# Three transposition banks and one sum bank in the attention stage, and first operands made while the last projection unit still runs

## The chip, the cores and the metric

One core of a Trainium2 chip runs the whole kernel. The metric is the device time of one launch in microseconds (us), the median over several executions. Engines are called as the profile calls them: PE is TensorE's matrix array and PEld its weight loads, ACT is ScalarE, DVE is VectorE, POOL is GpSimd, SP is the queue that issues most transfers. PSUM, where PE writes, has eight banks of 128 partitions by 512 float32.

## The reference, cut to what matters

One layer of a decoder for 1024 tokens of 1024 channels. What the change touches is the projection and the attention:

```python
h = rmsnorm(x, norm_mix_g)
proj = h @ w_in        # q | k_c v_c | k_s v_s | k_w v_w | gates | conv b, c, u
# 8 heads of 64 in 2 key/value groups; per query three branches:
#   compressed blocks (63 of them), selected blocks (all 16, so plain causal), window of 512
s = q*scale @ k.T - slope * distance;  p = masked_softmax(s);  o_branch = p @ v
o_attn = g0 * o_c + g1 * o_s + g2 * o_w
x = x + [rmsnorm(o_attn) | rmsnorm(o_conv)] @ w_out
x = x + (silu(dwconv3(h2 @ w_gate) + b) * (h2 @ w_up)) @ w_down     # h2 = rmsnorm(x)
```

## The kernel before, in words

**Precision.** Large matrix products run in a fast float32 form. An operand is split into a high part (an ACT copy that rounds) and a low part (a DVE subtraction of the high part from the operand), and products are summed over the parts. So every operand that is made costs an ACT instruction and then a DVE instruction that waits for it.

**Projection.** `w_in` is cut into 23 units of 128 output columns, numbered 0 to 22. A unit is 8 tiles (`unit_tile`, L486 to L496) of 6 matmuls each, one tile for each 128 rows of the contraction. All units read the normalised input from `R1`: tile `kt` reads `R1[kt]` (high) and `R1[8 + kt]` (low). A unit writes a pair of banks, number `n % 3`, and `evac` (L1276) on DVE multiplies it out of PSUM. Units 12 to 15 are queries, 16 the gates, 17 and 18 the compressed keys and values, 19 and 20 keys and values of group 0, 21 and 22 those of group 1. Between units 21 and 22 PE does the hidden layer of the compression.

**Attention operands.** `QA`, `QB`, `KA`, `KB`, `VT1`, `VT2`, `EX` lie in `R1`, the memory that the projection reads; `VT0` and group 1's keys lie in the weight slots `wh`, `wl`. `QA` holds queries (high and low), `QB` queries again with 20 rows of position terms below them, which two POOL transfers bring for queries and keys (L803, L804). Each engine makes its share (POOL L792, ACT L968, L976, L978, L987, L993, DVE L1367, L1368, L1381, L1387, L1394). In the kernel before, all of it waits for the end of unit 22 (`unit_done >= N_IN`), since any of it may lie in a slot that unit 22 still reads. DVE makes the low queries of heads 1 to 3 and the low values between the first four row maxima.

**Attention.** Work comes in blocks of 128 queries of one group (`BLOCKS`, 26 of them), 4 units each (one for a head; 104 units). For unit U: PE computes scores (L1831, L1832, masks L1843) into bank pair `U % 2` (banks 0 to 3), DVE takes row maxima (L1421), ACT exponentials (L1033). `scores(U)` waits for the exponentials of U - 2. While the units of a block run, each engine also handles the steps of the block before it, interleaved by `steps_behind`. A step is one tile of 128 keys for the four heads; there are 148 steps in 48 groups, and a group is one branch of one row of blocks. For step s PE transposes exponentials (L1879, 4 of them) into a ring of banks, ACT copies the high part out (L1044), DVE makes the low part (L1462, which frees the bank, semaphore `t_used`), and two steps later PE multiplies with the values (L1899, L1900) into the group's sum bank. When the group is complete, ACT copies the sum out (L1051), PE transposes it back (L1908) in a bank of the same ring, DVE adds the halves (L1448), and POOL weighs and adds the branches (L822, L827, L830). In the kernel before, banks 4 and 5 are the ring and banks 6 and 7 alternate as sum bank:

```python
PV_LAG, COPY_LAG, TURN_LAG, SQUARE_LAG = 2, 3, 6, 10
# turn_step(s):  pe.wait_ge(t_used, at - 1)        L1877
# values(s):     pe.wait_ge(t_used, T_OF[s] + 1)   L1887
#                pe.wait_ge(ot_copied, group - 1)  L1889, first step of a group
```

The order on every engine is fixed by these loops. A lag L means: done when step s + L is handled. Behind the attention, PE starts the output projection, whose tiles partly cover the last group's way out.

Of the kernel before, what the change touches and what calls it, by code (L numbers as in the profile page):

```python
# [27 lines left out]
ALU = mybir.AluOpType  # L28
# [3 lines left out]
P = 128  # L32
D = 1024
T = 1024
# [120 lines left out]
PV_LAG, COPY_LAG, TURN_LAG, SQUARE_LAG = 2, 3, 6, 10  # L155
# [18 lines left out]
PLAIN = [False for _ in STEPS]  # L174


def split_upto(s):
    return PLAIN[:s + 1].count(False)


def plain_before(s):
    return max([k + 1 for k in range(s) if PLAIN[k]], default=0)


# [19 lines left out]
def hybrid_layer(nc, xT, w_units, w_cmp1, w_cmp2, params_d, consts_d, masks_d, alibi_q, alibi_k, outT):  # L204
    with ExitStack() as ctx:
# [81 lines left out]
        VT1 = piece((2 * TT + 1) * P).rearrange("p (j d) -> p j d", d=P)  # L287
        VT2 = piece(2 * P).rearrange("p (j d) -> p j d", d=P)
        EX = piece(2 * BANK).rearrange("p (a b) -> p a b", a=2)
# [21 lines left out]
        EP = F1[:, K0 + 2, 0:BANK]  # L311
# [46 lines left out]
        x_in, aq_in = [sem(f"x_in{k}") for k in range(KT)], sem("aq_in")  # L358
# [409 lines left out]
        def _(pool):  # L768
# [15 lines left out]
            pool.wait_ge(unit_done, N_IN)  # L784

            def query_tiles(g, half, h):
                tiles = slice(half * TT // 2, (half + 1) * TT // 2)
                return tiles, F1[0:DH, Q0 + 2 * g + h // 2, :].rearrange("p (i q) -> p i q", q=P)[:, tiles, :]

            def queries_again(g, half, h):  # L790
                tiles, src = query_tiles(g, half, h)
                nc.gpsimd.tensor_scalar(QB[0:DH, tiles, h, :], src, DH ** -0.5, None, ALU.mult).then_inc(qb_even, 1)  # L792

            def queries(g, half, h):

                tiles, src = query_tiles(g, half, h)
                if g:
                    pool.wait_ge(sc_ready, FREE_Q[1 + half])
                nc.gpsimd.tensor_scalar(QA[0:DH, tiles, h, :], src, DH ** -0.5, None, ALU.mult).then_inc(qp_hi, 1)
# [1413 lines left out]
```

## Time and profile before

| what | value |
|---|---|
| time of the kernel before, median of 3 runs | 1434.09 us (1432.82 to 1435.97) |
| profiled execution, its own time | 1430.31 us |
| its span, first to last instruction | 1428.5 us |
| mean granted TensorE clock | 0.978 |
| PE busy | 1327.5 us, 93% |
| DVE busy | 868.8 us, 61% |
| ACT busy | 577.7 us, 40% |
| POOL busy | 332.3 us, 23% |
| attention, first scores to last values | 294.39 to 624.85 us |

The profile shows one execution. Engines run side by side, so busy shares do not add up to the span. A wait is put down to the instruction that came last. The granted clock is 1.00 where PE runs at 2.4 GHz and 0.50 where it runs at 1.2 GHz; a stretch with a number between has some of each. Matmul durations are those of one instruction from start to end; back to back, matmuls overlap, and the distance of their starts is what a sequence of them costs.

### The profile page before, as it was taken

How to read it: one execution, taken by the hardware profiler on the slowest of the kernel's cores; microseconds unless marked ns; L12 is line 12 of the kernel's file. 1: busy time of each engine (PE TensorE's matmuls, PEld its weight loads, DVE VectorE, ACT ScalarE, POOL GpSimd, SP SyncE). 2: the span in 40 equal slices, each digit the busy share in tenths (PEclk: the TensorE clock that was granted, in tenths of full speed). 3: DMA queues.
4: the chain of work that ended last, by engine and by line, in shares of the span. 5: the costliest groups of instructions: out<-in, count | busy, mean ns of one | idle time of the engine just before them, and what ended most of it. 6: DMA issues, size and time to landing. Idle time of an engine off the chain costs nothing.

```text
span 1428.5 us, 17091 instructions
## 1 busy us (share of the span) xinstructions
PE 1327.5 (93%) x6366; PEld 1078.7 (76%) x6366; DVE 868.8 (61%) x1195; ACT 577.7 (40%) x1028; POOL 332.3 (23%) x247
## 2 busy tenths in 40 slices
PE   7999999968688889879997999999999999999996
PEld 6788888856566667657886788888888878888885
DVE  6333432178677888755338877777888873335442
ACT  6211111067666876734154333333333333334330
POOL 0001000032121221110036554455554510002010
PEclk9999999979989999999998999999999999999998
DMA  5111111000000000043210222122222228444631
GB/s 214 51 44 59 45 59 74 0 19 1 1 1 1 1 1 1 1 177 104 88 45 30 103 89 84 64 89 89 89 89 89 74 86 320 169 128 145 217 100 59
DMA packets 37917, 110.75 MB, mean 78 GB/s; under 512 B 3988, under 2 KB 4500, under 8 KB 37652
## 3 DMA queue, kind: packets, MB, share of 16 engines
q1 hardware_dynamic: 37552, 108.83, 21.6%
q0 software_dynamic: 288, 0.90, 0.3%
q8 instruction: 48, 0.79, 0.2%
q14 instruction: 29, 0.24, 0.1%
HBM read 90.01 MB, written 19.92 MB: 77 GB/s over the span
## 4 chain that ended last, share of the span: by engine, by line
PE 69%; DVE 16%; ACT 7%; issue 7%; DMA 1%; POOL 1%; DVEq 0%; ACTq 0%; SPq 0%; POOLq 0%
PE PS L491 8%; PE PS L492 8%; PE PS L495 8%; PE PS L2019 6%; PE PS L2021 6%; PE PS L2020 6%; PE PS L2031 6%; PE PS L2033 6%; PE PS L2032 6%; DVE wl L1551 3%; DVE nmax L1421 3%; PE PS L1879 3%; ACT F L1033 2%; DVE ER L1462 2%; ACT ER L1044 1%
## 5 line engine op out<-in xcount | busy, mean ns | idle before, releaser
L491 PE MATMUL PS<-R,wh 128*128 128x512 f32 x560 | 222.4, 397 | 13.9 <-DVE wl L483 13.9
L492 PE MATMUL PS<-R,wh 128*128 128x512 f32 x560 | 219.8, 392 | 0.0
L2019 PE MATMUL PS<-R,wh 128*128 128x512 f32 x480 | 188.7, 393 | 13.4 <-DVE wl L1551 8.3
L2020 PE MATMUL PS<-R,wh 128*128 128x512 f32 x480 | 187.5, 391 | 0.0
L2021 PE MATMUL PS<-R,wl 128*128 128x512 f32 x480 | 187.5, 391 | 0.0
L495 PE MATMUL PS<-R,wl 128*128 128x512 f32 x560 | 173.5, 391 | 0.0
L2031 PE MATMUL PS<-R,wh 128*128 128x512 f32 x352 | 137.5, 390 | 0.0
L2033 PE MATMUL PS<-R,wl 128*128 128x512 f32 x352 | 137.0, 389 | 0.0
L2032 PE MATMUL PS<-R,wh 128*128 128x512 f32 x352 | 137.0, 389 | 0.0
L491 PEld LDWEIGHTS PS<-R,wh 128*128 128x128 f32 x560 | 106.0, 189 | 37.8 <-DVE wl L483 14.7
L495 PEld LDWEIGHTS PS<-R,wl 128*128 128x128 f32 x560 | 106.1, 189 | 22.6
L492 PEld LDWEIGHTS PS<-R,wh 128*128 128x128 f32 x560 | 106.1, 189 | 22.4 <-issue 0.7
L2019 PEld LDWEIGHTS PS<-R,wh 128*128 128x128 f32 x480 | 90.6, 189 | 36.5 <-DVE wl L1551 11.6
L1153 ACT ACTIVATE wh<-F 128x512 fp32r<-128x512 f32 x110 | 67.5, 625 | 111.2 <-PE PS L2021 99.5
L1879 PE MATMUL PS<-consts,F 128*128 128x128 f32 x528 | 84.2, 283 | 25.7 <-DVE ER L1462 7.5
L2021 PEld LDWEIGHTS PS<-R,wl 128*128 128x128 f32 x480 | 90.5, 189 | 19.0
L2020 PEld LDWEIGHTS PS<-R,wh 128*128 128x128 f32 x480 | 90.7, 189 | 18.5
L1421 DVE TENSOR_REDUCE nmax<-PS 128x1 f32<-128x64 f32 (+6 forms) x192 | 96.0, 538 | 13.5 <-PE PS L1843 12.1
L1551 DVE TENSOR_TENSOR wl<-F,wh 128x512 fp32r<-128x512 f32 x110 | 92.7, 851 | 5.0 <-ACT wh L1153 5.0
L1033 ACT ACTIVATE F<-PS,nmax 128x640 f32<-128x640 f32 (+7 forms) x128 | 89.2, 702 | 8.1 <-DVE nmax L1421 7.9
L1462 DVE TENSOR_TENSOR ER<-PS,ER 128x512 fp32r<-128x512 f32 (+1 forms) x99 | 68.1, 688 | 38.4 <-ACT ER L1044 37.1
L822 POOL TENSOR_TENSOR PBm<-PBm,factor 128x256 f32<-128x256 f32 x48 | 29.4, 613 | 265.8 <-DVE PBm L1448 265.4
(222 smaller groups left out, 2454.0 us busy)
## 6 DMA issues: line engine op xcount, KB each, us to landing
raw<-in_w_units SPq DMA_DIRECT2D x70, 512.0 KB, 3.6
F<-in_w_units SPq DMA_DIRECT2D x32, 512.0 KB, 4.1
gated<-F SPq DMA_DIRECT2D x22, 512.0 KB, 2.6
F<-gated SPq DMA_DIRECT2D x44, 256.0 KB, 3.6
F<-in_xT SPq DMA_DIRECT2D x16, 512.0 KB, 9.0
F<-in_w_units SPq DMA_DIRECT2D x12, 384.0 KB, 3.2
residual<-F SPq DMA_DIRECT2D x8, 512.0 KB, 2.6
F<-residual SPq DMA_DIRECT2D x8, 512.0 KB, 6.3
```

What stands on the lines that cost most here:

```text
L491: nc.tensor.matmul(out, w_h, hi(kt)[:, cols], start=first, stop=False)
L492: nc.tensor.matmul(out, w_h, lo(kt)[:, cols], start=False, stop=False)
L495: last = nc.tensor.matmul(out, w_l, hi(kt)[:, cols], start=False, stop=end)
L1421: last = nc.vector.tensor_reduce(nmax[:, br, i, h:h + 1], pair(U % 2)[:, col:col + count], AX.X, ALU.max, negate=True)
L1551: nc.vector.tensor_tensor(product_slot(wl, n), block_of(m, PRODUCTS[q][0]), f32(product_slot(wh, n)), ALU.subtract)\
L1879: last = nc.tensor.transpose(PS[0:rows, 4 + at % 2, h * P:(h + 1) * P], e_cols(n, br, h, j), ident)
L2019: nc.tensor.matmul(out, w_h, operand(name, k, 0), start=fresh and k == 0, stop=False, skip_group_check=not fresh)
L2020: nc.tensor.matmul(out, w_h, operand(name, k, 1), start=False, stop=False, skip_group_check=not fresh)
L2021: last = nc.tensor.matmul(out, w_l, operand(name, k, 0), start=False, stop=k == 3, skip_group_check=not fresh)
L2031: nc.tensor.matmul(out, w_h, a_part(n, 0), start=first, stop=False)
L2032: nc.tensor.matmul(out, w_h, a_part(n, 1), start=False, stop=False)
L2033: return nc.tensor.matmul(out, w_l, a_part(n, 0), start=False, stop=end)
```

## The change

Two edits in one. First, the banks: exponentials are transposed into a ring of three banks (4, 5, 6), and a single bank (7) collects the sums of every group. The lags of copying out, transposing back and squaring become 2, 4 and 8, and ACT copies a group's sum out before the exponentials of that place and not behind them. Second, the last projection unit: value transposes for group 0 move ahead of unit 22, the compressed values' matmuls into it, and unit 22 counts each finished tile in `r1_free`. `R1` is laid out anew, query pieces are split in halves, so that the first query half is free after 3 tiles (`Q_FREE`), group 0's keys after 5 (`K_FREE`), and the last values after 7 (`V2_FREE`). ACT, DVE and POOL make the first queries, keys and values at these counts. DVE multiplies unit 22 out (`evac(22)`) behind them. The transfer of the query rows is split in two, the second behind unit 22. A switch that was off everywhere (`PLAIN`) goes.

```diff
-PV_LAG, COPY_LAG, TURN_LAG, SQUARE_LAG = 2, 3, 6, 10
+PV_LAG, COPY_LAG, TURN_LAG, SQUARE_LAG = 2, 2, 4, 8
+T_RING, T_BANK, O_BANK = 3, 4, 7
...
-        QA = piece(GROUP * T).rearrange("p (i h q) -> p i h q", h=GROUP, q=P)
-        QB = piece(GROUP * T).rearrange("p (i h q) -> p i h q", h=GROUP, q=P)
-        KA = [piece(KEYS), flat(wh[:, :, :])[:, 0:KEYS]]
-        KB = [piece(KEYS), flat(wl[:, :, :])[:, RING * 1024 - KEYS:]]
+        def tiles_read(start, end):
+            return max(c // 1024 % KT for c in range(start, end)) + 1
+
+        QA, QB, KA, KB = [], [], [], []
+        QA.append(query_piece())
+        KA.append(piece(KEYS))
+        K_END = at_r[0]
+        QA.append(query_piece())
+        VT1 = piece((2 * TT + 1) * P).rearrange("p (j d) -> p j d", d=P)
+        QB_START = at_r[0]
+        QB.append(query_piece())
+        Q_FREE = max(tiles_read(0, GROUP * T // 2), tiles_read(QB_START, at_r[0]))
+        KB.append(piece(KEYS))
+        K_FREE = max(tiles_read(GROUP * T // 2, K_END), tiles_read(at_r[0] - KEYS, at_r[0]))
+        QB.append(query_piece())
...
@@ gpsimd
-            pool.wait_ge(unit_done, N_IN)
-            pool.wait_ge(qkv_ready, 4)
-            pool.dma_start(flat(QB[DH:DH + 2 * AR, :, :, :].rearrange("r i h q -> r i (h q)")), alibi_q).then_inc(aq_in, 16)
-            pool.dma_start(KB[0][DH:DH + 2 * AR, :], alibi_k[0]).then_inc(ak_in[0], 16)
-            queries_again(0, 0, 0)
-            for g in range(KV):
+            pool.wait_ge(qkv_ready, 2)
+            pool.wait_ge(r1_free, Q_FREE)
+            query_rows(0)
+            queries_again(0, 0, 0)
             queries_again(0, 0, 2)
+            pool.wait_ge(r1_free, K_FREE)
+            pool.dma_start(KB[0][DH:DH + 2 * AR, :], alibi_k[0]).then_inc(ak_in[0], 16)
+            key_pads(0)
+            pool.wait_ge(unit_done, N_IN)
+            query_rows(1)
+            key_pads(1)
             pool.dma_start(KB[1][DH:DH + 2 * AR, :], alibi_k[1]).then_inc(ak_in[1], 16)
@@ scalar
-            act.wait_ge(unit_done, N_IN)
+            act.wait_ge(qkv_ready, 8)
+            values_hi(slice(0, 2))
+            act.wait_ge(r1_free, Q_FREE)
+            for h in range(GROUP):
+                queries(0, 0, h)
+            act.wait_ge(r1_free, K_FREE)
             for half in range(2):
                 keys(0, half, 0)
-            queries(0, 0, 0)
             compressed_keys(0)
-            for h in range(1, GROUP):
-                queries(0, 0, h)
-            values_hi()
+            act.wait_ge(r1_free, V2_FREE)
+            act.wait_ge(v_lo, 2)
+            values_hi(slice(2, 3))
+            compressed_values()
@@ scalar, copy_out and behind
-                nc.scalar.activation(OT[group % 2], PS[:, 6 + group % 2, :], ACT.Copy).then_inc(ot_copied, 1)
+                nc.scalar.activation(OT[group % 2], PS[:, O_BANK, :], ACT.Copy).then_inc(ot_copied, 1)
                 if s < NS:
                     split_step(s)
+                if s - COPY_LAG in LAST_OF:
+                    copy_out(LAST_OF[s - COPY_LAG])
                 if unit is not None:
                     exponentials(unit)
                 if s in VALUES_AT:
                     later_values_hi(s)
-                if s - COPY_LAG in LAST_OF:
-                    copy_out(LAST_OF[s - COPY_LAG])
@@ vector
-            evac(22, 0, 0, 0, F1[:, 10, :])
+            values_lo(slice(0, 2))
+            for h in range(GROUP):
+                queries(0, 0, h)
             for half in range(2):
                 keys(0, half, 0)
-            queries(0, 0, 0)
             compressed_keys(0)
+            evac(22, 0, 0, 0, F1[:, 10, :])
...
-                if U < 3:
-                    queries(0, 0, U + 1)
                 if U == 1:
-                    values_lo()
-                if U == 2:
+                    values_lo(slice(2, 3))
                     compressed_values()
@@ tensor
-            pe.wait_ge(masks_in, 16)
+            pe.wait_ge(qkv_ready, 9)
             for t in range(TT):
                 last = nc.tensor.transpose(PS[:, 4 + t // 4, (t % 4) * P:(t % 4 + 1) * P], F1[:, V0, t * P:(t + 1) * P], ident)
             last.then_inc(vt_ready, 1)
+            pe.wait_ge(unit_lo, N_IN)
+            for kt in range(KT):
+                last = unit_tile((N_IN - 1) % RING, (N_IN - 1) % 3, h_hi, h_lo, kt, kt == 0, kt == KT - 1)
+                last.then_inc(unit_done if kt == KT - 1 else r1_free, 1)
+                if kt == 4:
+                    compressed_values()
@@ tensor, scores
                 if U == 0:
-                    pe.wait_ge(aq_in, 16)
-                    pe.wait_ge(clear_ready, 2 * KV)
+                    pe.wait_ge(aq_in[0], 16)
+                    pe.wait_ge(qkv_ready, N_QKV - 1)
+                if U == 1:
                     pe.wait_ge(qkv_ready, N_QKV)
@@ tensor, turn_step and turn_out
-                    pe.wait_ge(t_used, at - 1)
+                    pe.wait_ge(t_used, at - T_RING + 1)
@@ tensor, values
-                if s == first and group > 1:
-                    pe.wait_ge(ot_copied, group - 1)
-                elif s == first and group == 1:
+                if s == first and group:
+                    pe.wait_ge(ot_copied, group)
+                elif s == first:
                     pe.wait_ge(vc_lo, KV)
-                out, v = PS[:, 6 + group % 2, :], value_tile(g, br, j)[rows, :]
+                out, v = PS[:, O_BANK, :], value_tile(g, br, j)[rows, :]
```

## Rows read from the trace of the kernel before

**Rows 1.** Windows: stretch, its length, busy PE, PEld, DVE, ACT, POOL (counts), clock, DMA.

```profile
288.00:308.00 20.00, 9.73 (x51) 8.20 (x50) 13.27 (x33) 11.30 (x39) 10.48 (x13) 0.56 0.16 34
...
312.00:626.00 314.00, 263.36 (x1658) 203.45 (x1657) 242.14 (x456) 221.87 (x536) 62.19 (x84) 0.97 0.00 1
```

**Rows 2.** Timeline 276 to 295 us: start, duration, engine, line [idle before it].

```profile
276.09 0.50 PE L491 MATMUL PS<-R,wh 128*128 128x512 f32 x1
...
287.15 1.03 PE L1797 MATMUL PS<-consts,F 128*128 128x128 f32 x8
...
287.42 1.23 DVE L1279 TENSOR_TENSOR F<-PS,F 128x1024 f32<-128x1024 f32 x1 [9.35 <-PE PS L495]
...
290.55 1.52 POOL L792 TENSOR_SCALAR R<-F 64x512 fp32r<-64x512 f32 x1
290.66 1.08 DVE L1368 TENSOR_TENSOR R<-F,R 64x512 fp32r<-64x512 f32 x1
...
294.39 0.50 PE L1831 MATMUL PS<-R 128*128 128x192 f32 x1 [6.21 <-DMA R<-in_alibi_k]
```

**Rows 3.** The chain that ended last, 295 to 306 us: start, duration, what.

```profile
295.81 0.62 DVE nmax L1421 x3
...
296.46 0.70 DVE R L1381
...
297.21 0.53 PE PS L1831
...
304.98 0.32 ACT EC L1033
305.30 0.71 ACT F L1033 x4
```

**Rows 4.** Single lines of code: count, duration min/median/max in ns, first and last start.

```profile
L976 ACT ACTIVATE R<-F x10: 626/627/630, 288.7 to 493.0; 64x512 fp32r<-64x512 f32 x10
...
L1381 DVE SCALAR_TENSOR_TENSOR R<-F,R x16: 684/685/1128, 291.8 to 499.8; 64x512 fp32r<-64x512 f32 x16
...
L1051 ACT ACTIVATE F<-PS x48: 580/598/647, 317.6 to 624.9; 128x512 f32<-128x512 f32 x48
```

**Rows 5.** Transfers issued from 280 to 300 us: KB each, us from issue to landing.

```profile
R<-in_alibi_k POOLq DMA_DIRECT2D x1, 165.0 KB, 5.7
wl<-in_alibi_k POOLq DMA_DIRECT2D x1, 165.0 KB, 3.3
```

**Rows 6.** Timeline of PE: the first scores of unit 4 and of unit 8.

```profile
304.05 0.62 PE L1831 MATMUL PS<-R 128*128 128x320 f32 x1
...
313.36 0.47 PE L1831 MATMUL PS<-R 128*128 128x448 f32 x1 [0.87 <-ACT F L1033]
```

**Rows 7.** What PE waited for, 312 to 626 us: us in total, times, longest.

```profile
PE PS L1879 <- DVE ER L1462: 12.7, 15, 2.4
...
PE PS L1879 <- DVE R L1401: 5.2, 2, 3.4
PE PS L1899 <- ACT F L1051: 4.8, 5, 1.9
...
PE PS L1908 <- DVE R L1462: 0.7, 3, 0.4
```

**Rows 8.** Timeline at 398 to 400 us, where one group's sums end and the next begin.

```profile
398.54 0.60 ACT L1044 ACTIVATE ER<-PS 128x512 fp32r<-128x512 f32 x1 [0.17 <-PE PS L1879]
398.57 0.39 PE L1900 MATMUL PS<-ER,VT 128*128 128x512 f32 x1
...
399.33 0.50 PE L1899 MATMUL PS<-R 63*128 63x512 f32 x1
```

**Rows 9.** Windows of 2 us each, columns as in rows 1.

```profile
336.00:338.00 2.00, 2.00 (x9) 1.53 (x8) 1.70 (x3) 1.38 (x3) 0.00 (x0) 0.50 0.00 0
...
382.00:384.00 2.00, 0.25 (x4) 0.21 (x3) 1.02 (x2) 1.44 (x4) 0.00 (x0) 1.00 0.00 0
...
424.00:426.00 2.00, 2.00 (x9) 1.60 (x8) 0.69 (x2) 1.62 (x4) 1.92 (x3) 0.50 0.00 0
```

More of the change, by code:

```diff
@@ L173 @@
 KEYS_DONE = 34
[L174 to L182, printed above, removed]
 def steps_behind(unit):
@@ L357, in hybrid_layer @@
                                                        sem("tapr_ready"))
-        x_in, aq_in = [sem(f"x_in{k}") for k in range(KT)], sem("aq_in")
+        x_in, aq_in = [sem(f"x_in{k}") for k in range(KT)], [sem("aq_in0"), sem("aq_in1")]
+        r1_free = sem("r1_free")
         x1_in, out_done = sem("x1_in"), sem("out_done")
@@ L975, in queries @@
                 src = F1[rows, Q0 + 2 * g + h // 2, :].rearrange("p (i q) -> p i q", q=P)[:, tiles, :]
-                nc.scalar.activation(QA[rows, tiles, h, :], src, ACT.Copy, scale=DH ** -0.5).then_inc(q_hi, 1)
+                nc.scalar.activation(QA[half][rows, :, h, :], src, ACT.Copy, scale=DH ** -0.5).then_inc(q_hi, 1)
                 if h % 2:
-                    nc.scalar.activation(QB[0:DH, tiles, h, :], src, ACT.Copy, scale=DH ** -0.5).then_inc(qb_odd, 1)
+                    nc.scalar.activation(QB[half][0:DH, :, h, :], src, ACT.Copy, scale=DH ** -0.5).then_inc(qb_odd, 1)
             def hidden(kv):
@@ L1043, in split_step @@
                     act.wait_ge(pv_done, s - ER_RING + 1)
-                nc.scalar.activation(EH[s % ER_RING][rows, :], PS[rows, 4 + T_OF[s] % 2, :], ACT.Copy).then_inc(hi_ready, 1)
+                nc.scalar.activation(EH[s % ER_RING][rows, :], PS[rows, T_BANK + T_OF[s] % T_RING, :], ACT.Copy).then_inc(hi_ready, 1)
             def copy_out(group):
@@ L1380, in queries @@
                     dve.wait_ge(qp_hi, later)
-                nc.vector.scalar_tensor_tensor(QA[other, tiles, h, :], F1[rows, Q0 + 2 * g + h // 2, :]
+                nc.vector.scalar_tensor_tensor(QA[half][other, :, h, :], F1[rows, Q0 + 2 * g + h // 2, :]
                                                .rearrange("p (i q) -> p i q", q=P)[:, tiles, :], DH ** -0.5,
-                                               f32(QA[rows, tiles, h, :]), ALU.mult, ALU.subtract).then_inc(q_lo, 1)
+                                               f32(QA[half][rows, :, h, :]), ALU.mult, ALU.subtract).then_inc(q_lo, 1)
             def compressed_keys(g):
@@ L1793, in _ @@
                     last.then_inc(gt_ready, 1)
-            pe.wait_ge(masks_in, 16)
-            for t in range(TT):
-                last = nc.tensor.transpose(PS[:, 4 + t // 4, (t % 4) * P:(t % 4 + 1) * P], F1[:, V0, t * P:(t + 1) * P], ident)
-            last.then_inc(vt_ready, 1)
             def compressed_values():
@@ L1805, in compressed_values @@
                 last.then_inc(kvc_ready, 1)
+            pe.wait_ge(qkv_ready, 9)
+            for t in range(TT):
+                last = nc.tensor.transpose(PS[:, 4 + t // 4, (t % 4) * P:(t % 4 + 1) * P], F1[:, V0, t * P:(t + 1) * P], ident)
+            last.then_inc(vt_ready, 1)
+            pe.wait_ge(unit_lo, N_IN)
[4 more added lines that the diff above has]
+                    compressed_values()
+            pe.wait_ge(masks_in, 16)
             def scores(U):
@@ L1830, in part @@
                     out = PS[:, bank, col:col + count]
-                    nc.tensor.matmul(out, QA[:, i, h, :], KA[g][:, key:key + count], start=True, stop=False)
-                    return nc.tensor.matmul(out, QB[0:DH + 2 * AR, i, h, :], KB[g][0:DH + 2 * AR, key:key + count], start=False,
+                    nc.tensor.matmul(out, QA[i // WT][:, i % WT, h, :], KA[g][:, key:key + count], start=True, stop=False)
+                    return nc.tensor.matmul(out, QB[i // WT][0:DH + 2 * AR, i % WT, h, :], KB[g][0:DH + 2 * AR, key:key + count], start=False,
                                             stop=not masked)
@@ L1894, in values @@
                 rows = slice(0, NCMP if br == CMP else P)
-                out, v = PS[:, 6 + group % 2, :], value_tile(g, br, j)[rows, :]
-                if PLAIN[s]:
-                    nc.tensor.matmul(out, f32(v), EP[rows, :], start=s == first, stop=s == end).then_inc(pv_done, 1)
-                    return
+                out, v = PS[:, O_BANK, :], value_tile(g, br, j)[rows, :]
                 nc.tensor.matmul(out, v, EH[s % ER_RING][rows, :], start=s == first, stop=False)
```

71 lines of the change are left out of this document (36 added, 35 removed).

## The prediction, made before the changed kernel was built or run

> **What bounds the kernel now.** The page comes first: PE is busy 93% of the span, so time is won only where PE idles or runs at half clock. Windows over the attention stage say where that is. From 288 to 308 us PE is busy 9.7 of 20 us at a mean clock of 0.56; from 312 to 626 us it is busy 263.4 of 314 us, so it idles 50.6 us, while DVE is busy 77% and ACT 71% [rows 1]. No engine is full there, so the stage is held by waits for one another as much as by work. Then the timeline of the first stretch: projection and value transposes end at about 288.2 us, and the first scores start at 294.39 us, released by the position rows of the keys [rows 2]. Behind them the chain of waits goes round three engines, scores on PE, maxima on DVE, low queries of the next head on DVE, scores again, and a round is 294.39 to 297.21, 2.82 us [rows 2, 3]. Last the list of what PE waited for from 312 to 626 us: seven rows (transposes L1879 and L1908 behind DVE, the first and last of them are shown) make 43 waits of 35.3 us in all. They are waits for a transposition bank. Five waits, 4.8 us, are for the copy of a group's sum [rows 7].
>
> **The front, step by step.** Unit 22 is 48 matmuls from 276.09 to 287.15 us, 11.06 us or 1.38 us a tile; the eight transposes last 1.03 us [rows 2]. In the new order transposes run from 276.1, the unit from 277.1, and the four small matmuls of the compressed values inside it are taken as 0.3 us (fewer and smaller than the eight transposes). Three tiles are done at 281.3, five at 284.0, the unit at 288.5. PE therefore finishes its part when it did before, and nothing is lost there.
>
> ACT makes four high queries and two copies, 6 x 0.63 us [rows 4], from 281.4 to 285.2, then two halves of keys to 286.5, compressed keys and values to about 287.7. DVE follows each: the low queries are done at about 285.9. Both key halves on DVE lasted from the end of its evacuation, 287.42 + 1.23, to 290.66 + 1.08, or 3.1 us [rows 2]; from 285.8, when the first high half exists, they end at 288.9, the compressed ones at 289.1. POOL issues the query rows at 281.4 (0.6), copies two heads (1.5 to 1.7 each, one shown [rows 2]) and issues the key rows at 285.2. Alone, such a transfer of 165 KB took 3.3 us; behind the 320 KB of queries 5.7 [rows 5]. The queries' half is issued 3.8 us earlier, so I take 3.3: landed at 288.5. Before, the key rows were issued as the transposes ended, at 288.2, took 5.7, and the first scores started at 294.39, 0.5 us after landing [rows 2, 5]. Two paths so meet at 289.1; the first scores start 5.3 us earlier.
>
> Then DVE has to do the evacuation of unit 22, which it used to do first: 289.1 + 1.2 = 290.3. Behind it stand the first maxima, and unit 1's scores wait for it too. From there maxima 0.65, exponentials 1.03 (0.32 + 0.71) [rows 3]: unit 2's scores start at 292.0. No low query stands between maxima any more, so a round of two units is scores 0.71 (they lay 1.42 us, 294.39 to 295.81, at half clock), maxima 0.62, exponentials 1.03, handing over 0.1: 2.5 us. Unit 4's scores start at 294.5 and not at 304.05 [rows 6]: 9.6 us. Units 4 to 7 took 9.3 us, to 313.36 [rows 6], mostly at half clock; ACT then sets their pace, and I credit two scores on the chain at full clock, 2 x 0.71 = 1.4. **The front gives 11.0 us.**
>
> This rests on the clock staying up. PE fell to half clock after it had idled 6.2 us. Later it fell about 334 to 339, 369 to 373, 392 to 397 and 421 to 427 us, each time behind a wait of 1.9 to 3.4 us; five windows of 2 us show 0.50, first and last are in rows 9. In the window 382 to 384 PE was busy 0.25 of 2 us and the clock stayed [rows 9]. In the new front no wait should be over 1 us. If it falls all the same, each of two rounds is 0.7 longer and the 1.4 is lost: 8.2 us. That is the lower bound of the front; the upper one, with evacuation not in the way, 12.2.
>
> At one place a rule speaks against this front. POOL's query copies now lie beside DVE's low queries. In the trace a subtraction on DVE that began 0.11 us after such a POOL copy took 1.08 us, and the median of the low queries is 0.685, so it cost 0.4 us and did not last to the copy's end (290.55 + 1.52) [rows 2, 4]. I go by that. The Trainium skill (SBUF — State Buffer, Who interferes with whom) says that a DVE instruction with two SBUF inputs and a GpSimd one that reads SBUF block each other for the whole instruction. By that rule DVE's low queries would wait for both POOL copies, to 285.2, and the front would give about 9 us where the rows give 11.0.
>
> **The ring of three.** Before, `turn_step(s)` waits for the same low part as `values(s - 2)` right behind it. With a third bank the four transposes go ahead and the wait meets the values. So a wait shrinks by no more than four transposes issued back to back, 0.47 us, estimated as half of eight (1.03) [rows 2] less the overlap of their ends. 43 waits x 0.47 would be 20 us; many are shorter, and with each cut at 0.47 they add up to 16 us. Not all of it stays: PE that comes earlier meets ACT and DVE still at work. DVE's 77% leaves room, so I keep somewhat over half, 9 us. Bounds 0 and 16.
>
> **One sum bank.** Waits for the copy (4.8 us [rows 7]) had the copy stand three steps behind and behind exponentials; it moves ahead of both, and I take 4 of them as gone. In return each group's first sum waits for the copy of the group before, 47 times. How long is read at each boundary: last sum ends 398.96, ACT's high part that stands ahead of the copy ends 399.14, copy 0.6 [rows 4, 8], so 399.77, and the next sum started at 399.33: 0.44 us late [rows 8]. Worked out so at all 47 boundaries, 7 are late, 3.1 us in all; at the others scores or a transposition back lie between and cover the copy by 0.1 to 2.7 us. With PE's other waits gone cover shrinks: I take 5 us. Were every boundary as bare as this one, it would be 47 x 0.44 = 21 us. That is the upper bound, 3 the lower. The copy ahead of the exponentials holds these up by 0.6 us where a unit begins; the scores behind them rarely wait for it, and I take 1 us. Moving POOL's and DVE's ends of a group two steps forward costs nothing: their instructions are the same, and POOL is idle most of the stage. The later values (L1401, 5.2 us in two waits [rows 7]) are among the 43.
>
> **Clock in the stage.** Four dips of some 4 to 6 us at half clock cost about half of each, 8 to 10 us together. The one at 369 us stands behind a wait for a copy (1.9 us [rows 7]) that should vanish, others get shorter: 3 us, bounds 0 and 6. The end of the attention is the same chain as before, with the one boundary of 0.2 us more.
>
> **Sum.** 11.0 + 9 + 4 - 5 - 1 + 3 - 0.2 = 20.8 us, from the profiled execution's 1430.31 us to 1409.5. That execution lay 3.8 us under the median of 1434.09; with the same difference on the median the forecast is 1413 us.
>
> **Rivals.** (1) Both parts pay, as above: chance 0.6, 1403 to 1421 us. (2) Only the front pays; the ring's waits move whole to the values and what the copy gives, the single bank takes: 1434 - 11 = 1423, range 1420 to 1427, chance 0.18. For it: in-order PE waits at the values for the very low part it waited for before. Against: DVE and ACT idle a quarter of the stage, partly waiting for those transposes. Its neighbour in the Trainium skill (TensorE: Matmul & The Clock Gate, HAM oscillation) is a kernel in which more PSUM buffering gave nothing; here 43 waits for a bank are in the trace, so I give it no more. (3) The front is made too late: POOL and DVE block each other, key rows land late and the clock falls behind the gap. Front 6, stage 8: 1420, chance 0.08. (4) The clock stays at full through the whole stage and the front: 10 us more from (1), 1403 or less, down to 1396, chance 0.09. (5) Slower: the single bank holds PE at every boundary for the whole copy path. The gains to be eaten are 11 + 9 + 4 + 3 = 27 us, so it decides from 27 / 47 = 0.57 us a boundary; with high part and copy both in the way (0.6 + 0.6 less 0.2 of transposes not covered) it is 1.0 x 47 = 47 us, 1454 us. Against it: the 0.44 at a bare boundary. Chance 0.05.
>
> **Numbers.** Cases 1, 3, 4 and most of 2 lie from 1401 to 1427; this is the range, with 0.1 outside on each side. A measurement tells 0.2%, 2.9 us, from no change. Faster 0.91, within 0.2% 0.05 (front at its low bound and the bank at 20 us), slower 0.04.
>
> **What would show it.** Right: first scores at 289 us, unit 4's at 294 to 295, clock 1.00 from 288 to 312; the 35.3 us of waits for a bank down to under half, those of the values for DVE up; waits of L1899 for L1051 under 6 us; the stage from unit 8 to the last values shorter by some 9 us. Wrong: a gap of several us before the first scores with half clock behind it; L1899 waiting for L1051 at most of 47 boundaries; a stage as long as before with its waits only renamed.

## The result, and the profile after

The changed kernel takes 1391.12 us (median of 4 runs, 1389.27 to 1392.53) against 1433.45 us for the kernel before (4 runs, 1432.53 to 1435.97) on the same chip: ratio 0.9701, interval 0.9682 to 0.972, or 42.3 us less. The forecast was 1413 us, and the time lies under its range. The profiled execution took 1392.53 us, against 1430.31 for the profiled one before: these two are 37.8 us apart and not 42.3, as the one before lay under its median and this one over it. What follows splits the 37.8. First the page: busy times and the granted clock over 40 slices.

```profile
PE 1318.5 (95%) x6366; PEld 1076.2 (77%) x6366; DVE 863.5 (62%) x1195; ACT 576.2 (41%) x1028; POOL 332.6 (24%) x248
...
PEclk9999999999999999999999999999999999999998
```

Then windows over the front and the stage (columns as in [rows 1]). The stage here runs from the first to the last values, 302.48 to 585.35 us; before, 311.79 to 624.85.

```profile
288.00:308.00 20.00, 15.61 (x99) 12.85 (x98) 14.52 (x45) 14.01 (x53) 6.92 (x8) 0.83 0.08 20
292.00:296.00 4.00, 2.54 (x18) 2.25 (x18) 1.55 (x9) 3.17 (x18) 4.00 (x3) 0.86 0.09 15
296.00:300.00 4.00, 3.98 (x20) 3.33 (x19) 3.16 (x11) 2.30 (x9) 0.30 (x1) 0.50 0.00 0
302.48:585.35 282.87, 253.74 (x1656) 201.36 (x1653) 236.83 (x456) 219.50 (x534) 62.43 (x84) 0.99 0.00 1
```

The same for the stage of the kernel before, from its own first values to its last:

```profile
311.79:624.85 313.06, 262.42 (x1656) 202.69 (x1653) 242.14 (x456) 221.47 (x535) 62.19 (x84) 0.97 0.00 1
```

The first values start 9.3 us earlier, and the stage is 30.2 us shorter. Its 1656 matmuls are the same, so the 30.2 split in two: PE idles 29.1 us and not 50.6 (21.5 less), and is busy 253.7 us and not 262.4 (8.7 less). What follows the stage is 1.8 us longer. How much of the 8.7 is the clock can be read: windows over the stretches in which the granted clock was 0.50, their sum for the kernel before (four stretches) and for ring_of_two below (six), the one stretch of the changed kernel, and the sum of its second profiled execution, after_again (two):

```profile
sum 17.00, PE 15.80 PEld 12.98 DVE 10.05 ACT 8.30 POOL 3.16; mean PE 3.95 PEld 3.24 DVE 2.51 ACT 2.07 POOL 0.79
sum 20.60, PE 20.00 PEld 17.33 DVE 12.66 ACT 9.73 POOL 4.76; mean PE 3.33 PEld 2.89 DVE 2.11 ACT 1.62 POOL 0.79
448.50:455.30 6.80, 6.71 (x29) 5.39 (x30) 4.79 (x12) 4.44 (x15) 0.00 (x0) 0.50 0.00 0
sum 13.70, PE 13.49 PEld 10.38 DVE 10.19 ACT 8.89 POOL 2.53; mean PE 6.74 PEld 5.19 DVE 5.09 ACT 4.44 POOL 1.27
```

Work at half clock takes about twice the time (four transposes 1.06 us at 300.32 and 0.60 at 302.12), so half of PE's busy time there is the clock's price: 7.9 us before and 3.4 in the changed kernel. The clock gave back 4.5 us, and in the second execution of the same changed kernel only 1.2. The other 4 us of the 8.7 lie at full clock. An estimate that would explain them: the list of what PE waited for has 69 waits in the stage before and 39 now, and at every break the end of a matmul lies bare (it lasts 0.39 us where the next follows after 0.23), 30 x 0.16 = 4.8 us. No run tests that. The forecast had 11.0 for the front, 7 for waits in the stage and 3 for its clock: the stage gave three times its share.

What PE waited for in that stage, to be held against [rows 7]:

```profile
PE PS L1919 <- ACT F L1069: 10.5, 14, 1.6
PE PS L1854 <- ACT F L1053: 6.8, 8, 2.1
PE PS L1902 <- DVE PBm L1466: 3.7, 4, 1.5
...
PE PS L1902 <- DVE R L1474: 1.1, 1, 1.1
PE PS L1928 <- DVE R L1474: 1.0, 1, 1.0
PE PS L1928 <- DVE ER L1474: 0.9, 3, 0.4
PE PS L1902 <- DVE R L1416: 0.2, 1, 0.2
```

L1902 and L1928 are the transposes forth and back (L1879 and L1908 before), L1919 the values, L1854 the scores, L1069 the copy of a sum, L1053 the exponentials, L1474 and L1416 low parts, L1466 the halves. Waits for a transposition bank went from 43 with 35.3 us to 10 with 6.9. No row says that the values (L1919) wait for a low part (L1474): the waits did not move there. Values waiting for the copy rose from 4.8 to 10.5 us, scores waiting for exponentials from 3.5 to 6.8.

Where the 28 us of bank waits had been is seen behind a transposition back. Timeline of the kernel before, 449.5 to 451.7 us, two rows of PE's with the work between them:

```profile
449.56 0.63 PE L1908 MATMUL PS<-consts,F 128*128 128x128 f32 x4 [0.18 <-DVE ER L1462]
...
449.83 0.59 ACT L1044 ACTIVATE R<-PS 128x512 fp32r<-128x512 f32 x1
...
450.45 0.69 DVE L1462 TENSOR_TENSOR R<-PS,R 128x512 fp32r<-128x512 f32 x1 [1.04 <-ACT R L1044]
...
451.29 0.63 PE L1879 MATMUL PS<-consts,F 128*128 128x128 f32 x4 [1.10 <-DVE R L1462]
```

The same group's sum in the changed kernel, timeline 419.3 to 420.7 us:

```profile
419.39 0.61 PE L1928 MATMUL PS<-consts,F 128*128 128x128 f32 x4
...
419.83 0.60 PE L1902 MATMUL PS<-consts,F 128*128 128x128 f32 x4
...
420.19 0.47 PE L1919 MATMUL PS<-R,VT 128*128 128x512 f32 x1
```

Before, the transposition back took one of two ring places. The next step therefore needed the other, the bank of the step *just before it*, and waited for all of that step: its high part on ACT, its low part on DVE. From one start to the other 1.73 us passed. With three places it needs the bank of the step before that, free long since: 0.44 us. In the kernel before, 18 of the 43 waits, 17.9 us, stand at steps directly behind a transposition back, each for a low part; in the changed kernel one does, 1.1 us (three more, 2.2 us, wait there for halves). The numbering of ring places in the kernel, laid beside the trace, sorts the other 25 too: two steps wait for a place that later values held (5.2 us), six steps for one that a transposition back held (3.4), 13 waits are of transpositions back themselves (6.6). Only 4 waits, 2.2 us, are of a step for the step two before it.

Last the front, from its timeline:

```profile
282.24 0.58 POOL L806 DMA_DIRECT2D R<-in_alibi_q  x1 [108.26 <-PE PS L500]
282.37 4.33 DVE L1396 SCALAR_TENSOR_TENSOR R<-F,R 64x512 fp32r<-64x512 f32 x4 [1.51 <-ACT R L991]
...
282.85 3.47 POOL L795 TENSOR_SCALAR R<-F 64x512 fp32r<-64x512 f32 x2
...
286.28 0.55 POOL L820 DMA_DIRECT2D R<-in_alibi_k  x1
...
289.10 1.23 DVE L1295 TENSOR_TENSOR F<-PS,F 128x1024 f32<-128x1024 f32 x1
...
289.86 0.33 PE L1854 MATMUL PS<-R 128*128 128x192 f32 x1 [0.80 <-DMA R<-in_alibi_k]
...
292.50 0.33 PE L1854 MATMUL PS<-R 128*128 128x192 f32 x1 [1.23 <-ACT F L1053]
...
295.05 0.64 PE L1854 MATMUL PS<-R 128*128 128x320 f32 x1 [0.85 <-ACT F L1053]
```

First scores at 289.86 (forecast 289.1), unit 2's at 292.50 (292.0), unit 4's at 295.05 (294.5). The key rows were issued 1.1 us later than forecast and took 3.1 us to land: 0.8 us of it because POOL's issue of the query rows started at 282.24 and not at 281.4, 0.3 because its two copies took 3.47 us and not 3.2. The clock did not stay: 0.50 from 296 to 300.

### The profile page after: what moved, and what is told of

Its sections match the earlier page's. It is cut to its first block, busy times and chain, and to the rows that moved or that the text cites. A ratio compares the mean times of both kernels' runs of the same rounds, so it can differ in the third digit from the quotient of the medians.

```text
span 1390.7 us, 17095 instructions
## 1 busy us (share of the span) xinstructions
PE 1318.5 (95%) x6366; PEld 1076.2 (77%) x6366; DVE 863.5 (62%) x1195; ACT 576.2 (41%) x1028; POOL 332.6 (24%) x248
## 4 chain that ended last, share of the span: by engine, by line
PE 74%; DVE 13%; issue 6%; ACT 5%; POOL 1%; DMA 1%; DVEq 0%; SPq 0%; ACTq 0%; POOLq 0%
PE PS L496 9%; PE PS L497 8%; PE PS L500 8%; PE PS L2037 6%; PE PS L2039 6%; PE PS L2038 6%; PE PS L2049 6%; PE PS L2051 6%; PE PS L2050 6%; PE PS L1902 3%; DVE wl L1560 3%; ACT F L1053 2%; PE PS L1919 2%; DVE nmax L1439 2%; PE PS L1854 2%
## 5 line engine op out<-in xcount | busy, mean ns | idle before, releaser
L1053 ACT ACTIVATE F<-PS,nmax 128x640 f32<-128x640 f32 (+7 forms) x128 | 89.5, 704 | 12.3 <-DVE nmax L1439 12.1
L1902 PE MATMUL PS<-consts,F 128*128 128x128 f32 x528 | 81.9, 278 | 7.9 <-DVE PBm L1466 3.7
L1474 DVE TENSOR_TENSOR ER<-PS,ER 128x512 fp32r<-128x512 f32 (+1 forms) x99 | 67.8, 686 | 29.6 <-ACT ER L1062 28.9
```

Of the source, the lines that this page charges most:

```text
L1902: last = nc.tensor.transpose(PS[0:rows, T_BANK + at % T_RING, h * P:(h + 1) * P], e_cols(n, br, h, j), ident)
```

## The experiments

Ratios are to the kernel before on the same chip. Each expectation names its own theories. The question under all of them: is the gain that was not forecast the third transposition bank's, and which of its users', or is it the sum bank's, the copy order's or the lags'?

### The parts alone

**front_only**: the changed kernel with its bank part undone.

```diff
-PV_LAG, COPY_LAG, TURN_LAG, SQUARE_LAG = 2, 2, 4, 8
-T_RING, T_BANK, O_BANK = 3, 4, 7
+PV_LAG, COPY_LAG, TURN_LAG, SQUARE_LAG = 2, 3, 6, 10
+T_RING, T_BANK, O_BANK = 2, 4, 6
...
-                out, v = PS[:, O_BANK, :], value_tile(g, br, j)[rows, :]
+                out, v = PS[:, O_BANK + group % 2, :], value_tile(g, br, j)[rows, :]
... (values wait for the copy of group - 2, and the copy stands behind the exponentials)
```

> The changed kernel with its bank part undone: two transposition banks, two alternating sum banks, lags 3, 6, 10 and the copy behind the exponentials, as before. Only the new order around unit 22 is left. Theory A (the front gives what the trace after shows at the first sums, 311.79 to 302.48, and the stage behind it does not change): 1433.5 - 9.3 = 1424 us, and the list of waits of the stage as before, some 50 us. Theory B (part of the stage's 30 us comes from the front, because PE enters it at full clock and with its operands made): 1410 to 1418 us.

Measured 1421.39 us (1418.51 to 1425.32), ratio 0.9934 (0.991 to 0.9957). First values at 301.32, and then the stage and waits of the kernel before (1.5 us shorter, with 51.7 us of idle time):

```profile
PE PS L1902 <- DVE ER L1474: 13.1, 15, 2.4
PE PS L1902 <- DVE R L1474: 8.0, 8, 2.0
...
301.32:612.90 311.58, 259.93 (x1656) 200.42 (x1653) 241.46 (x456) 221.32 (x536) 62.40 (x84) 0.98 0.00 1
```

The front is worth 9.5 us by the ratio, 11.2 by the medians. The forecast's 11.0 holds.

**banks_only**: the kernel before with the bank part alone (ring, sum bank, lags, copy ahead of the exponentials).

```diff
-PV_LAG, COPY_LAG, TURN_LAG, SQUARE_LAG = 2, 3, 6, 10
+PV_LAG, COPY_LAG, TURN_LAG, SQUARE_LAG = 2, 2, 4, 8
+T_RING, T_BANK, O_BANK = 3, 4, 7
...
-                    pe.wait_ge(t_used, at - 1)
+                    pe.wait_ge(t_used, at - T_RING + 1)
...
```

> The kernel before with the bank part alone: ring of three, one sum bank, lags 2, 4, 8, copy ahead of the exponentials. The front is as before. Theory A (parts add up): 1433.5 - 42.3 + 9.3 = 1400 us. Theory B (the stage gains from the front): 1406 to 1414 us. If my forecast of 9.8 us for this part had been right on its own, 1424 us.

Measured 1399.95 us (1398.87 to 1402.51), ratio 0.9779 (0.9748 to 0.981): 32 us. The stage lasts 283.20 us, its waits are those of the changed kernel (10.7 us for the copy). 9.5 and 31.7 us by the ratios make 41.2 of 42.8: the parts add up, and the error is in the bank part, forecast at 9.8.

### Whose bank it was

**ring_of_two**: all else as changed, but transposes forth and back and later values share banks 4 and 5.

```diff
+BANK_AT, FREE_AT, HELD = {}, {}, {}
+for at_tile in range(len(T_OF) + len(O_OF) + len(V_OF)):
+    is_step = at_tile in set(T_OF.values())
+    bank_at = (4 + at_tile % 2) if is_step else (4 + at_tile % 2)
+    BANK_AT[at_tile], FREE_AT[at_tile] = bank_at, HELD.get(bank_at, 0)
+    HELD[bank_at] = at_tile + 1
...
-                    pe.wait_ge(t_used, at - T_RING + 1)
+                    pe.wait_ge(t_used, FREE_AT[at])
```

> The changed kernel with everything in a ring of two banks (4, 5) and bank 6 unused; one sum bank, lags and copy order as changed. Theory A: the 18 waits behind a transposition back come again (17.9 us, and the slow clock behind some of them), while the earlier copy stays: 1391 + 18 to 28 = 1409 to 1419 us. Theory B (slack as forecast, at most 16 us): 1400 to 1407 us. Were the single sum bank dear, it would be slower than the run with the front alone (1424 us).

Measured 1416.98 us (1415.62 to 1419.81), ratio 0.9905 (0.9871 to 0.9938). The third bank is worth 25.9 us beside the changed kernel by the medians, 29 by the ratios. The waits:

```profile
PE PS L1910 <- DVE ER L1482: 11.9, 13, 2.0
PE PS L1910 <- DVE PBm L1474: 8.8, 14, 1.5
PE PS L1910 <- DVE R L1424: 5.1, 2, 2.6
...
302.20:611.24 309.04, 264.03 (x1656) 204.34 (x1653) 240.58 (x456) 221.41 (x535) 62.16 (x84) 0.97 0.00 1
```

(L1910 is the transposition forth, L1482 the low part, L1474 the halves, L1424 the later values' low part.) 12 waits, 13.2 us, are directly behind a transposition back. A later one, beside its like in the changed kernel: back at 443.78, forth at 445.23, 1.45 us; there 427.37 and 427.81, 0.44 us. The stage's idle time is 45.0 us against 29.1, its busy time 264.0 against 253.7: of 26 us, 16 are waits and 10 a longer busy time. The clock is 6.6 of the 10 (20.00 us of PE's work at half clock against 6.71, and half of the difference), and 3.3 against after_again; the rest lies at full clock.

**side_bank**: steps alternate on banks 4 and 5; bank 6 takes only transpositions back and later values. So a step has no more slack than before, but nobody cuts into its ring.

```diff
 # as in ring_of_two, but:
+    bank_at = (4 + [a for a in sorted(T_OF.values())].index(at_tile) % 2) if is_step else (6)
```

> The changed kernel, but steps turn in a ring of only two banks (4, 5), and bank 6 is kept for the transpositions back and the later values. Theory A: before, 18 waits of 17.9 us stood at the transposes right behind a transposition back, because that one had taken a place in the ring and the next step then needed the bank of the step just before it, with ACT's and DVE's whole way (1.3 us) in between. What the third bank gives is mostly that the transposition back no longer takes such a place. Then this kernel is as fast as the changed one: 1391 to 1395 us. Theory B: the third bank gives slack at every step, as I forecast (at most 0.47 us a wait). Then taking it from the steps loses over half of the gain of the ring: 1402 us or more.

Measured 1395.57 us (1393.57 to 1399.82), ratio 0.9755 (0.9718 to 0.9791), 21.4 us under ring_of_two and 4.5 over the changed kernel. Transposes forth (L1910) wait for low parts seldom and shortly now; what waits is the transposition back (L1936), for the one bank that it shares with its like and whose halves are not yet added:

```profile
PE PS L1936 <- DVE PBm L1474: 7.6, 8, 1.6
...
PE PS L1910 <- DVE ER L1482: 2.6, 6, 0.8
```

This decides it: some 21 us come from taking the other tiles out of the steps' ring (both runs were taken on one chip), and a rest of 3 to 8 (4.5 by the medians, 7.7 by the ratios, 2.5 to 4.5 by the length of the stage) from three places that all share. Only such slack for the steps had I priced.

**own_bank**: ring of two for steps and later values, and each transposition back goes into its own group's sum bank, 6 or 7. For it lags are 2, 2, 3, 7, PE turns back behind the values, and DVE adds the halves behind the low part of that place and no longer ahead of it.

```diff
-PV_LAG, COPY_LAG, TURN_LAG, SQUARE_LAG = 2, 2, 4, 8
+PV_LAG, COPY_LAG, TURN_LAG, SQUARE_LAG = 2, 2, 3, 7
...
+for at_group, at_tile in O_OF.items():
+    BANK_AT[at_tile] = 6 + at_group % 2
...
-                    pe.wait_ge(ot_copied, group)
+                    pe.wait_ge(t_used, O_OF[group - 2] + 1)
```

> Ring of two banks (4, 5) for steps and later values, two alternating sum banks (6, 7), and the transposition back goes into the sum bank from which the sum has just been copied, at lag 3 and behind that step's values. The front as changed. So no transposition back takes a place in the ring, with no bank more than before. Theory A (the place in the ring was the cost): the 17.9 us behind transpositions back stay away, waits for the copy go too, about 16 single steps wait 0.5 to 0.8 us for the halves to be added: 1387 to 1396 us. Theory B (three banks for steps are what counts): 1402 us or more.

Measured 1415.47 us (1412.26 to 1418.06), ratio 0.9877 (0.9858 to 0.9896). The forecast of the time missed. The waits behind a transposition back did go (one is left, 1.0 us), and steps (L1910) wait for low parts (L1482) only 4.2 us where it was 14.4 in ring_of_two. But the sum bank now comes free only with the halves:

```profile
PE PS L1927 <- DVE PBm L1474: 15.8, 10, 3.0
PE PS L1910 <- DVE R L1424: 6.7, 2, 4.2
...
302.87:613.55 310.68, 267.49 (x1656) 209.64 (x1654) 240.44 (x456) 221.59 (x535) 68.69 (x86) 0.94 0.00 1
```

One shared place was exchanged for another, and as three orders changed with it, its time tells nothing for or against the place in the ring; side_bank does.

### One sum bank, its copy and the lags

**two_sums_early**: ring of two as in ring_of_two, two sum banks as before, with the new lags and copy order.

```diff
 # the ring as in ring_of_two, and:
-                out, v = PS[:, O_BANK, :], value_tile(g, br, j)[rows, :]
+                out, v = PS[:, 6 + group % 2, :], value_tile(g, br, j)[rows, :]
-                    pe.wait_ge(ot_copied, group)
+                    pe.wait_ge(ot_copied, group - 1)
```

> Ring of two banks for everything, two alternating sum banks as before, but the changed lags (2, 4, 8), the copy ahead of the exponentials, and the changed front. Beside the run with the front alone (1421.4) it has only order and lags changed; beside the run with a ring of two and one sum bank (1417.0) only the second sum bank added. Theory A (the earlier copy pays by itself, the single bank costs what its waits cost, some 3.5 to 5 us as forecast): 1411 to 1414 us. Theory B (the copy order only repairs what the single bank breaks, and is worth nothing with two): 1420 to 1423 us.

Measured 1420.01 us (1417.1 to 1421.65), ratio 0.9907 (0.9878 to 0.9936). The same as ring_of_two (0.9905) and front_only (0.9934) within their intervals: with a ring of two neither the second sum bank nor order and lags are worth anything that can be measured.

**copy_late**: the changed kernel with the copy behind the exponentials again.

```diff
-                if s - COPY_LAG in LAST_OF:
-                    copy_out(LAST_OF[s - COPY_LAG])
                 if unit is not None:
                     exponentials(unit)
                 if s in VALUES_AT:
                     later_values_hi(s)
+                if s - COPY_LAG in LAST_OF:
+                    copy_out(LAST_OF[s - COPY_LAG])
```

> The changed kernel, only that ACT copies a group's sum out behind the exponentials again, not ahead of them. Theory A: the order is what makes one sum bank cheap. Where a unit begins at that step (some half of 47 places), the copy stands behind 1 to 1.7 us of exponentials, and the next sum waits for it: the waits of the values for the copy grow from 10.5 us to 20 to 30, 1391 + 10 to 20 = 1401 to 1411 us. Theory B (my forecast priced the order at 1 us, for exponentials held up): 1390 us.

Measured 1413.03 us (1411.95 to 1414.95), ratio 0.987 (0.985 to 0.989), 22 us over the changed kernel.

```profile
PE PS L1919 <- ACT F L1069: 30.6, 30, 3.1
...
302.32:607.99 305.67, 263.09 (x1656) 210.96 (x1653) 239.71 (x456) 219.84 (x535) 62.44 (x84) 0.95 0.00 1
```

With one sum bank and a ring of three the copy's place carries 22 us; with two and a ring of two (above) none that could be measured. Of these 22, PE's idle time is 13.5 (42.6 against 29.1).

**lag_three**: the changed kernel with each lag behind the sums one longer.

```diff
-PV_LAG, COPY_LAG, TURN_LAG, SQUARE_LAG = 2, 2, 4, 8
+PV_LAG, COPY_LAG, TURN_LAG, SQUARE_LAG = 2, 3, 5, 9
```

> The changed kernel with the lags of copy, transposition back and squares one step longer (3, 5, 9), the copy still ahead of the exponentials. With one sum bank the next group's first sum stands at this very step behind two engines: ACT must make that step's high part before it copies. Theory A: each boundary waits up to one step longer, waits of the values for the copy from 10.5 to 25 us or more, 1403 to 1411 us. Theory B (cover from scores between absorbs it, as I read 40 of 47 boundaries): 1391 to 1395 us.

Measured 1476.06 us (1468.47 to 1478.46), ratio 1.031 (1.0283 to 1.0337): 85 us over the changed kernel, 43 over the one before, in the expected direction and far more than expected.

```profile
PE PS L1919 <- ACT F L1069: 62.6, 44, 3.2
...
303.08:662.54 359.46, 286.49 (x1656) 228.95 (x1653) 243.03 (x456) 221.34 (x534) 62.05 (x84) 0.88 0.00 1
```

The first values of a group stand on PE right behind the transposes of a step. With lag 3 the copy that they need stands on ACT behind the high part of that very step, so PE waits through high part and copy at nearly every boundary, 1.4 us on average, and the clock falls to 0.88. That is the mechanism of rival 5, one lag away.

**act_copy_first**: on ACT alone the copy goes ahead of the high part as well. **sum_first**: that, and on PE a group's last values go ahead of the transposes of their place.

```diff
 # both
+                if s - COPY_LAG in LAST_OF:
+                    copy_out(LAST_OF[s - COPY_LAG])
                 if s < NS:
                     split_step(s)
 # sum_first, on PE, ahead of turn_out and turn_step
+                early = s - PV_LAG in LAST_OF
+                if early:
+                    values(s - PV_LAG)
```

> The changed kernel, only that ACT copies a group's sum before the high part of that step and not behind it; PE's order is as changed (the run with the sum made first had both exchanges, and came out at 1394.9). ACT then waits some 0.2 to 0.5 us for the last sum where it used to work, and the copy is done 0.4 us sooner. Theory A: the waits of the values for the copy shrink from 10.5 to under 6 us and the time goes to 1386 to 1389 us; then PE's exchange was what hurt there. Theory B: ACT standing still for the sum delays high parts and exponentials by as much, 1392 to 1397 us; then ACT's exchange was what hurt.

> The changed kernel with one more exchange: at the step where a group's last sum is due, PE makes that sum before the next transposes and not behind them, and ACT copies it before the next high part. The copy then has two steps' transposes to hide behind. Theory A: most of the 10.5 us in 14 waits for the copy go: 1383 to 1388 us. Theory B: the last sum now waits for its own low part, which the transposes covered, and nothing is won: 1390 to 1394 us.

Measured 1399.59 us (1398.3 to 1400.42), ratio 0.9768 (0.9745 to 0.9791), and 1394.85 us (1391.93 to 1396.11), ratio 0.9742 (0.9723 to 0.976): neither is faster than the changed kernel, and act_copy_first is 8 us slower. In act_copy_first:

```profile
PE PS L1854 <- ACT F L1053: 9.2, 11, 2.2
PE PS L1902 <- DVE PBm L1466: 6.3, 7, 1.8
PE PS L1919 <- ACT F L1069: 4.4, 10, 1.1
```

The copy's waits fell by 6.1 us, the other two rose by 5.0, and the stage got 7 us longer: ACT works in order, and while it stands at a sum that isn't complete, high parts and exponentials stand behind it. In sum_first copies cost 5.7 us and scores 8.3.

### The clock of the front, and a control

**filled_front**: 8 transposes of the identity into bank 6, read by nobody, ahead of the scores of units 0, 2 and 4. This adds work, and nothing else but one wait ahead of the first of them.

```diff
+            pe.wait_ge(kcs_ready, 1)
+            def filler(count):
+                for _ in range(count):
+                    nc.tensor.transpose(PS[:, 6, 0:P], ident, ident)
+            filler(8)
             for U in range(NU + GROUP):
                 if U < NU:
                     scores(U)
+                if U in (1, 3):
+                    filler(8)
```

> The changed kernel with 24 transposes of a constant into bank 6, which is free there, in three gaps of PE before units 0, 2 and 4 (they add work and change no result). In the trace of the changed kernel the clock fell to half from about 295 to 303 us, though PE never waited over 1.3 us there. Theory A: filled gaps hold the clock at full; scores of units 4 to 7 take half the time: first sums 1 to 2.5 us earlier, 1389 to 1390 us. Theory B: ACT sets the pace there (busy 6.2 of 8 us) or the filling itself is in the way: 1391 us or up to 1 us more.

Measured 1390.63 us (1388.31 to 1393.81), ratio 0.9718 (0.9698 to 0.9738).

```profile
288.00:296.00 8.00, 7.35 (x65) 6.31 (x62) 4.84 (x21) 3.84 (x20) 6.92 (x8) 1.00 0.18 44
296.00:304.00 8.00, 5.28 (x40) 3.86 (x38) 6.71 (x19) 7.53 (x25) 0.00 (x0) 1.00 0.00 0
```

The clock stays at full from 288 to 304 us. The first values start at 300.47 and not 302.48, but its first scores were 0.6 us early already (289.29 against 289.86). From first scores to first values it is 11.2 us against 12.6, and 12.3 in after_again: the fall of the clock cost 1.1 to 1.4 us. In the time it can't be told from the changed kernel.

**after_again**: the changed kernel once more, beside two_sums_early and lag_three, with no edit.

> The changed kernel itself, unaltered, as a yardstick for the runs that came within a few us of it, on one chip with the two above: 1391 us and a ratio of 0.970 both by the earlier measurement; any theory says the same. If it comes out up to 3 us away, differences of that size between the runs of different calls mean nothing.

Measured 1391.69 us (1389.62 to 1394.9), ratio 0.9706 (0.968 to 0.9731), stage 284.89 us. Against it the stage of side_bank (287.35) is only 2.5 us longer, so the few us that are left for more slack are uncertain by about half; the 21 us are not. Its list of waits is that of the changed kernel within 0.6 us a row, but PE was busy 256.7 us and not 253.7 at a clock of 0.98 and not 0.99. A difference of 3 us in PE's busy time can so be one execution's.

## Why the prediction was wrong

| step | forecast | measured | by |
|---|---|---|---|
| front | 11.0 (8.2 to 12.2) | 9.5 to 11.2 | front_only |
| one sum bank, copy order, lags | 2 lost (4 - 5 - 1) | 0 to 4.4 gained, with a ring of two | ring_of_two against front_only |
| ring of three | 9 (0 to 16) | 26 to 29 with its clock, 16 of it idle time | ring_of_two against changed |
| clock in the stage | 3 (0 to 6) | 4.5 (1.2 against after_again) | PE's busy time at half clock, before against changed |

**The step that failed is "The ring of three".** It began: "`turn_step(s)` waits for the same low part as `values(s - 2)` right behind it". From that came "a wait shrinks by no more than four transposes issued back to back, 0.47 us", and the 9 and the bound of 16. The premise is true only where the ring's last two places were steps. Transpositions back and later values take places too, and behind one of them the count `at - 1` ends with the tile of step s - 1. There the wait is the whole way of a step through ACT and DVE, and a third bank removes it whole. Of the 43 waits that I cut by 0.47 each, only 4 with 2.2 us were of the kind that the premise describes. The row was at hand: seven rows in [rows 7], L1908 and L1401 among them, said that others used the ring, and waits of up to 2.4 us don't fit four transposes' worth of 0.47. Bank waits fell by 28.4 us where the cap was 16. Waits for copy and exponentials gave 9 back (5.7 and 3.3); the forecast kept about the right fraction, somewhat over half, of a gross that was too small.

**The clock** gave 4.5 us where I had 3, inside its bounds; what I had not priced is the other 4 us of PE's busy time. The four dips in the kernel before [rows 9] cost 7.9 us, at the lower end of my 8 to 10, and stand at long waits of four kinds: a step behind a transposition back (2.4 us), values behind a copy (1.9), a step for the place of later values (3.4), a transposition back itself (2.3). Three of the four so came from the second users of the ring. The changed kernel's one dip stands at a wait of scores for exponentials (2.1 us). That the waits cause the dips is shown in direction by own_bank, copy_late and lag_three, where long waits of other kinds bring the clock to 0.94, 0.95 and 0.88.

**One sum bank** cost nearly twice its price in waits: 10.5 us for the copy, where 5.8 were left by my terms (4.8 - 4 + 5), over the bound of 6 that I named. With a ring of two those waits are only 3.5 us, and there the single bank cost nothing measurable in time; what it costs beside a ring of three no run shows. And the copy ahead of the exponentials, booked as a loss of 1 us, is what the single bank stands on: 22 us. I had worked out the boundary for the new order only, and never what the old one would cost.

**The front** went as written, each milestone 0.5 to 0.8 us late. The first scores waited for the key rows, which POOL issued 1.1 us later than forecast. Most of that is no cost of this front but of the execution: in front_only, with the same front, POOL began at 281.23 and not 282.24, and the first scores started at 289.22. The first of its two copies took 2.00 us, which makes 0.3 us over the 3.2 that I had for both. DVE's four low queries took 0.69 to 1.43 us each, 4.24 in all, where four of the 0.685 of [rows 4] make 2.74. So the two engines did hold each other up, DVE by 1.5 us, but not whole: from 282.37 to 286.70 us both were busy (DVE 4.24, POOL 4.30 of 4.33 us), and one after the other 2.74 and two copies of 1.48, the median of POOL's eight, would be 5.7 us. The Trainium skill (SBUF — State Buffer, Who interferes with whom) has them lock each other out for the whole instruction; the trace agrees that they disturb each other, with these numbers, and not that one stands still until the other ends. DVE's delay lay beside the path: its key halves ended at 288.9, as forecast. Wrong was "In the new front no wait should be over 1 us", and with it that the clock would stay up: one wait was 1.23 us, and it fell, which cost 1.1 to 1.4 us (filled_front). For a clock that falls I had forecast 8.2 us for the front. It fell and the front gave 9.5 to 11.2, so that 11.0 holds is in part luck: I was wrong that the clock would stay and had its fall priced twice too high (2.8 us). In the kernel before the clock had fallen at about 290.6 us, well inside the idle stretch of 6.2 us and not behind it, as I had put it.

**The rivals.** Rival 2, waits that only move to the values, is out: no such row is there, and my own sign that those waits would go up failed with it (1.5 us before, none now). Its neighbour in the Trainium skill (TensorE: Matmul & The Clock Gate, HAM oscillation), where more PSUM buffering gave nothing, doesn't carry over: here one bank more gave 26 us. Rival 4 was nearest in time, but by another way: the clock in the front did fall. Rival 5's mechanism exists, at lag 3, for 43 us over the kernel before.

Left open is what the busy time at full clock is that went with the waits, and how much of the clock's part belongs to which wait. No run has three transposition banks and two sum banks, for which there is no ninth bank.

## What to carry to other kernels

When a wait is for a place in a ring, write down which tile held that place, for every kind of tile that uses the ring, before pricing the wait: a rare second user turns a distance of two into one, and that place costs the whole latency. An accumulator bank could be given up here, for more than it cost, because its copy stands early in the copying engine's order and its lag is right; moved by one place or one step, it costs 22 or 85 us. Removing waits also shortened PE's busy time, by 0.4 to 0.65 of the idle time that went (8.7 of 21.5, 10.3 of 15.9), and the clock is only a part of that: count it with the waits and not as a remainder.

## What the runs showed of the hardware that I had not expected

The clock fell in the new front without a long wait: PE was busy 2.54 of 4 us from 292 to 296, no wait was over 1.3 us, and from 296 to 300 it ran at 1.2 GHz (0.50), busy throughout. Before, in the window 382 to 384, PE was busy 0.25 of 2 us and stayed at 1.00 [rows 9]. So the length of the last wait alone does not tell whether the clock falls. With 24 small transposes added, PE was busy 7.35 of 8 us from 288 to 296 and the clock stayed at 1.00 to 304.
